# A two-layer encoder trunk: loading both embedding weights ahead of x, and taking rows 0-127 through the first projection first

## What is computed

```python
for i in range(DEPTH):                       # DEPTH = 2
    h = _rmsnorm(x, pre_norm_g[i])
    z = h @ w_in[i]                          # all groups' columns in one projection
    ...                                      # sparse and differential attention: oa, ob
    y = jnp.concatenate([oa * jax.nn.silu(ga), ob * jax.nn.silu(gb)], axis=-1) @ w_out[i]
    x = x + _rmsnorm(y, post_norm_g[i])
    gate = jax.nn.sigmoid(x @ w_ple_gate[i])
    e = (p[i] @ w_ple_proj[i]) * gate        # p: 256 rows by 256
    x = x + _rmsnorm(e, ple_norm_g[i])
```

## Time and profile before

| | |
|---|---|
| median of 3 runs | 394.84 us (394.23 to 395.21) |
| the profiled execution | 395.01 us |
| its span | 393.1 us |
| mean granted TensorE clock | 0.980 |
| PE busy | 367.1 us, 93% |
| DVE busy | 260.6 us, 66% |
| ACT busy | 222.3 us, 57% |
| POOL busy | 66.8 us, 17% |
| chain that ended last | PE 64%, DVE 11%, ACT 9%, DMA 5% |

### The profile page before, as it was taken

One profiled execution on the slowest core, in us unless ns is written; L12 is line 12 of the kernel. 1 busy time (PEld: TensorE's weight loads), 2 busy tenths in 40 slices (PEclk: granted clock), 3 DMA queues, 4 the chain that ended last, 5 costly groups with the idle time before them and its releaser, 6 DMA issues.

```text
span 393.1 us, 5602 instructions
## 1 busy us (share of the span) xinstructions
PE 367.1 (93%) x1932; PEld 301.6 (77%) x1932; DVE 260.6 (66%) x450; ACT 222.3 (57%) x451; POOL 66.8 (17%) x122
## 2 busy tenths in 40 slices
PE   6799999859999999999999999985999999999992
PEld 6597787748878788888888878774887878888882
DVE  2738697757766587588686579775666648757733
ACT  4838557662668645554674656766266855555321
POOL 1514331050400000003015513105041000000000
PEclk9999999997999999999999999999699999999998
DMA  7999735452455443667655753545235544352002
GB/s 267 303 234 334 251 96 174 136 159 81 111 155 166 158 162 111 182 214 138 204 171 173 252 160 91 178 131 161 84 99 170 160 162 154 113 179 90 0 23 85
DMA packets 32075, 61.64 MB, mean 157 GB/s; under 512 B 2384, under 2 KB 4688, under 8 KB 32048
## 3 DMA queue, kind: packets, MB, share of 16 engines
q1 hardware_dynamic: 30928, 58.01, 47.3%
q0 software_dynamic: 1120, 3.28, 4.1%
HBM read 60.23 MB, written 1.05 MB: 156 GB/s over the span
## 4 chain that ended last, share of the span: by engine, by line
PE 64%; DVE 11%; ACT 9%; DMA 5%; issue 5%; POOL 4%; SPq 1%; DVEq 0%; POOLq 0%; ACTq 0%
PE proj L932 17%; PE proj L933 17%; PE proj L934 17%; PE pv L1072 5%; DVE w_lo L689 4%; ACT w_hi L505 3%; DMA raw<-in_w_in_dram 3%; ACT probs L606 3%; DMA resid<-in_x_dram 2%; PE sc L974 2%; PE sc L1044 2%; PE tr L1057 2%; PE tr L990 1%; DVE score L767 1%; DVE neg_max L777 1%
## 5 line engine op out<-in xcount | busy, mean ns | idle before, releaser
L932 PE MATMUL proj<-w_hi,act_hi 128*128 128x512 f32 (+1 forms) x416 | 168.7, 406 | 0.9 <-DVE w_lo L689 0.8
L934 PE MATMUL proj<-w_hi,act_lo 128*128 128x512 f32 (+1 forms) x416 | 161.1, 387 | 0.0
L933 PE MATMUL proj<-w_lo,act_hi 128*128 128x512 f32 (+1 forms) x416 | 161.0, 387 | 0.0
L689 DVE TENSOR_TENSOR w_lo<-raw,w_hi 128x1024 fp32r<-128x1024 f32 (+1 forms) x108 | 129.2, 1212 | 38.8 <-ACT w_hi L505 38.2
L505 ACT ACTIVATE w_hi<-raw 128x1024 fp32r<-128x1024 f32 (+1 forms) x108 | 110.7, 1042 | 9.7 <-DMA raw<-in_w_in_dram 7.3
L932 PEld LDWEIGHTS proj<-w_hi,act_hi 128*128 128x128 f32 x416 | 79.0, 190 | 16.8 <-DVE w_lo L689 1.1
L934 PEld LDWEIGHTS proj<-w_hi,act_lo 128*128 128x128 f32 x416 | 78.8, 189 | 16.4
L933 PEld LDWEIGHTS proj<-w_lo,act_hi 128*128 128x128 f32 x416 | 79.1, 190 | 12.4
L606 ACT ACTIVATE probs<-sc,neg_max 128x128 f32<-128x128 f32 (+1 forms) x64 | 26.0, 426 | 31.1 <-DVE neg_max L777 31.1
L453 POOL TENSOR_TENSOR rstd<-var,minus_half 128x1 f32<-128x1 f32 x12 | 6.7, 556 | 192.1 <-DVE var L679 176.8
L1072 PE MATMUL pv<-v_all,pT 128*128 128x64 f32 (+1 forms) x144 | 20.5, 290 | 12.2 <-DVE qT_b L828 10.2
(11 more groups left out here) (124 smaller groups left out, 366.6 us busy)
## 6 DMA issues: line engine op xcount, KB each, us to landing
raw<-in_w_in_dram SPq DMA_DIRECT2D x64, 512.0 KB, 3.7
raw<-in_w_out_dram SPq DMA_DIRECT2D x16, 512.0 KB, 3.3
raw<-in_w_ple_gate_dram SPq DMA_DIRECT2D x16, 512.0 KB, 3.7
raw<-in_w_in_dram SPq DMA_DIRECT2D x8, 324.0 KB, 7.2
raw<-in_w_ple_proj_dram SPq DMA_DIRECT2D x4, 512.0 KB, 3.5
resid<-in_x_dram SPq DMA_DIRECT2D x2, 512.0 KB, 7.6
g_norm<-in_post_norm_g_dram POOLq DMA_DIRECT2D x2, 512.0 KB, 6.0
g_ple<-in_ple_norm_g_dram POOLq DMA_DIRECT2D x2, 512.0 KB, 7.5
```

The source lines that it names most:

```text
L689: nc.vector.tensor_tensor(w_lo[:, g % SLOTS, 0:nk * cols], raw[:, g % RAW_SLOTS, 0:nk * cols], w_hi[:, g % SLOTS, 0:nk * cols].bitcast(fp3 ...
L932: nc.tensor.matmul(ps, src_hi[:, b, k0 + k, :], hi, start=(first_u and k == 0), stop=False)
L933: nc.tensor.matmul(ps, src_hi[:, b, k0 + k, :], lo, start=False, stop=False)
L934: last = nc.tensor.matmul(ps, src_lo[:, b, k0 + k, :], hi, start=False, stop=last_k)
```

## The change

In SP's list of transfers the second embedding weight is put ahead of x's first block. The step "pre" is divided: "presq" holds ACT's part (the wait for x and the square), "pre" keeps the parts of DVE and POOL. In layer 0 all four embedding products come before the first transposes; block 0's square stands after mm(0,1), block 1's square after mm(1,1), and DVE's part of block 1's norm after the transposes of block 0. IDX then runs over units 2 to 5 for block 0, with block 1's transposes after unit 4, and then over units 2 to 5 for block 1. `START` is new for the first ten units. In layer 1 the two parts of "pre" stand next to each other, where "pre" stood.

```diff
-START = [1, 2, 5, 8, 11, 11, 16, 17, 18, 19]
+START = [1, 1, 7, 10, 11, 12, 15, 16, 18, 20]
...
     if L == 0:
-        out += [("pT", 0), ("pre", 0, 0)]
-        mms("PLE", ple, {0: [("pre", 1, 0)], 2: t8("h", 0), 3: t8("h", 1)})
-        mms("IDX", both, {})
+        out += [("pT", 0)]
+        mms("PLE", ple, {1: [("presq", 0, 0), ("pre", 0, 0)], 3: [("presq", 1, 0)] + t8("h", 0) + [("pre", 1, 0)]})
+        mms("IDX", one(0), {2: t8("h", 1)})
+        mms("IDX", one(1), {})
         mms("QB", both, {3: [("TI", 0)], 5: [("D", 0)]})
     else:
         out += [("ple0", 1, 1, L - 1)]
-        mms("PLE", ple, {0: t8("h", 0) + [("psq", 1, 1, L - 1), ("ple1", 1, L - 1)], 2: [("pre", 1, L)]})
+        mms("PLE", ple, {0: t8("h", 0) + [("psq", 1, 1, L - 1), ("ple1", 1, L - 1)], 2: [("presq", 1, L), ("pre", 1, L)]})
...
-                      12: ([("pre", 0, L + 1)] if L + 1 < DEPTH else []) + [("psq", 1, 0, L)]})
+                      12: ([("presq", 0, L + 1), ("pre", 0, L + 1)] if L + 1 < DEPTH else []) + [("psq", 1, 0, L)]})
...
-                if g == 0:
+                if g == 1:
                     load_x(0)
-                elif g == 1:
                     sp.dma_start(g_norm[:, :], pre_norm_g[0, :].partition_broadcast(P)).then_inc(gpre_in[0], 16)
                     load_x(1)
...
-                elif kind == "pre":
+                elif kind == "presq":
                     b, M = s[1:]
                     if M == 0:
                         act.wait_ge(x_in[b], 16)
```

## The result

| | before | after |
|---|---|---|
| median of 4 runs | 394.53 us (394.08 to 395.21) | 397.51 us (396.67 to 397.94) |
| profiled execution, its span | 395.01, 393.1 us | 396.67, 394.9 us |
| mean granted TensorE clock | 0.980 | 0.974 |

The ratio is 1.0072, with a 95% interval of 1.0056 to 1.0088: slower by 2.8 us by the ratio (3.0 between the two medians), where +1.7 was forecast.

The account below looks back on a forecast made before the run. TensorE, busy 93% of the span, was taken as the bound. Up to 1.0 us gained against 2.7 of new waits gave +1.73 us at the mark, carried to the end: 396.6 us, range 394.5 to 398.5.

Parts of the forecast that it names:

- The case that had half of the chances: The forecast itself: opening waits on PE move the end by +1.73 us to 396.6, own range 395.9 to 397.4; chance 0.50.
- Case C: Opening on PE: transposes and waits lower the clock, some 2 us on top of the waits, 398.7; chance 0.06.
- Case D: Unit 11's transfer lands late among POOL's loads, delaying TI's copy; D waits up to 2, likely 1: 397.7; chance 0.05.
- PE, embeddings; ACT, first rows: Opening: PE's 2.24 us gap goes, products end 13.6, not 17.0; square at 11.55; PE takes first norm at 14.87.
- ACT, second rows; DVE: Opening: square of rows 128-255 at 14.95; their norm at 19.5 to 20.8, delaying units 4 and 5's remainders behind it.
- the sum: Opening's total: up to 1.0 gained, 2.7 of new waits on PE; net +1.73 us.
- IDX and QB: PE after the embeddings: 0.9 us a half-unit, QB at 28.25 instead of 25.55, units 6 and 7 taking 5.47.
- The mark: Start on PE of QB's first product reading unit 8: 32.32 before, forecast 34.05; its shift moves the end equally.
- Case B: PE's two 5.12 us stalls: clock return gives 0.85 back twice, 395.0, chance 0.18; other way 398.3, 0.08.
- Case A: Opening: ACT and DVE less in the way, norm of rows 128-255 before 17.5, mark 31.35, 394.0; chance 0.10.
- Case E: SP's transfers: the swap does nothing, second weight lands at 9.3 as before, square 0.8 later: 397.4; chance 0.03.
- Layer 1: Second layer: both parts of "pre" adjacent, each engine's order the same, so no cost.

Follow-up runs that it names:

- experiment 2: after plus filler matmuls in PE's two opening gaps to keep the clock high; its 6-filler version, which gives QB at 28.46, measured 397.22 us, ratio 1.0058.
- swap_only: Kernel before with only the transfer swap, second embedding weight issued ahead of x's first block, step order as before; 395.34 us, ratio 1.0017.
- best version of experiment 7: early_sq_split plus filler matmuls ahead of PE's two long stalls; 387.49 us, ratio 0.9827 to before.
- after_fill20: after plus 20 filler matmuls on PE ahead of the 5.12 us wait in each layer; 392.85 us, ratio 0.9964 to before.
- sq_only: after with ACT's two squares alone moved ahead of the embedding copies that wait for PE, DVE's order kept; 397.53 us in one execution.
- early_sq_split: early_sq_hold, but the five small vectors issued after IDX's rotation of rows 128-255; 392.11 us, ratio 0.9931 to before.
- hold_loads: Kernel before with POOL's layer 0 loads issued only after QB's rotation of rows 128-255; 396.49 us, ratio 1.0052.
- early_sq_hold: after with squares early, norm of rows 128-255 ahead of unit 2's remainder, IDX alternating blocks, POOL's loads held; 394.18 us, ratio 0.9987.

## Why the prediction was right, and where it was off

The direction and the range held (397.51 in 394.5 to 398.5), and the forecast of +1.7 was too small by 1.1 us. The case that had half of the chances did not hold as it stood: 397.51 is above its own range (395.9 to 397.4), because two cases with 0.11 between them, C and D, came on top. Case C was priced at 398.7, outside of the stated range. That the time stayed inside is in part luck: C cost less than priced, and it and D overlap, as told below.

*PE, embeddings; ACT, first rows.* Right. Square at 11.57 (forecast 11.55), norm of rows 0-127 at 13.57 (13.55), transposes at 14.91 (14.87).

*ACT, second rows; DVE.* Right. Square 14.92 (14.95), norm of rows 128-255 19.34 to 20.62 (19.5 to 20.8), PE's wait for `act_lo` 1.41, then 1.03 for unit 4's remainder behind the norm (1.9 in the sum, less here because unit 3's products, at the low clock, took up a part of it).

*IDX and QB.* The term "0.9 us a half-unit" failed, because the rows it rests on were at the high clock. In after the matmuls of units 3 and 4 start 0.27 apart instead of 0.15. With the clock kept high, experiment 2 gives QB at 28.46, against 28.25 in the sum and 29.76 in after. The mark is then at 34.19, against 34.05 in the sum and 35.49 in after: 1.3 of the 1.4 us that the sum missed are the low clock's.

*Case C, the opening cools PE, 0.06.* It happened, at 1.3 us at TI instead of the 2 priced, and it deserved far more of the chance. I had written down 3.6 us of transposes and idleness, longer than the 2.24 us that left the clock alone, plus further waits, and yet called it unlikely. PE was idle for 1.15 and 1.41 us of it, with eight transposes in between, and the clock fell at about 19.0, after PE had resumed. The Trainium skill (TensorE: Matmul & The Clock Gate, Part 4) says that a transpose doesn't count as busy the way a matmul does. No run here settles that. In swap_only 2.65 us of idleness without a transpose lowered the clock too, so the idle time of after, 2.56 us in two parts, may be enough by itself. And in the best version of experiment 7, twelve transposes and an idle 1.45 us between the embedding products and unit 2 left the clock at 1.00:

```profile
13.64 1.03 PE L976 MATMUL sc<-ident,work 128*128 128x128 f32 x8
16.12 0.63 PE L976 MATMUL sc<-ident,work 128*128 128x128 f32 x4 [1.45 <-DVE act_lo L727]
16.82 0.39 PE L934 MATMUL proj<-w_hi,act_hi 128*128 128x324 f32 x1
```

*Case D, loads collide, 0.05.* It happened too. Unit 11's transfer took 10.1 us in after_fill20 and unit 11's copy started at 36.78 in after, with D at 38.43 just covered by PE; in sq_only D waited 1.63 us for it. The step that failed is "at the rate of before it lands at 33 to 34": while POOL's small vectors are in flight little is moved at a high share (80 GB/s at 0.87, as 38 at 0.78 in the earlier trace rows), so the bytes ahead are no measure of the time. That it is the small vectors and not POOL's large loads is seen in early_sq_split, where they were issued alone, from 31.15 to 34.1 us, the large loads from 40.91 on (columns as in rows 6):

```profile
36.00:38.00 2.00, 2.00 (x12) 1.60 (x11) 1.04 (x1) 1.28 (x2) 1.88 (x4) 1.00 0.97 28
```

The Trainium skill (Trainium Kernel Development and Optimization, Key Constraints) has all queues on the same 16 engines; hold_loads agrees, since unit 8 is no longer waited for once POOL's loads are out of its way.

C and D lie side by side, not in a row. In after TI's copy was ready for D at 38.22, held by unit 11, and PE's own work ended at about the same time, held back by the low clock. Where the low clock was absent or off PE's path, D was at 37.31, 37.48 and 38.13 in three executions, 0.3 to 1.1 us earlier and not 1.3, and the totals moved by 0.3 to 0.6. A version of after with both taken away and nothing else changed was not run.

*Case B, the clock gives it back.* It happened in the profiled execution. From the product behind the second layer's stall to the rotation's transposes it took 17.26 us in after (279.01 to 296.27) and 18.73 in before (275.83 to 294.56): 1.5 us less, hence the 1.7 of its total. Behind the first stall nothing was given back (18.47 in after, 18.30 in before). The medians don't show it (+3.0 with these stalls, +3.3 without their low clock), and behind the first stall the same stretch took 17.35 in early_sq_hold and 18.72 in early_sq_split, though each had one 5.12 us wait ahead of it. So it looks like a matter of the execution and not of the kernel; one profile of each kernel can't show it.

*Case A* did not occur: the norm ended at 20.62, not before 17.5. *Case E* did not either: the second weight's copy started at 8.07, in x's old place. *Layer 1*: the lag is 3.1 us at the first index product and 3.2 at the second layer's stall, so it cost nothing, as said.

## What to carry to other kernels

Before a step is put behind another on a busy engine, replay every engine's queue: here a copy that waits for PE came ahead of a square, and a norm with a round trip to POOL ahead of two weights, and the 2.24 us gap that went came back as waits of 1.15, 1.41 and 1.03. Durations from rows hold only at the clock of those rows: the clock stayed high behind an idle 2.24 us and fell behind 2.65, so a new gap of that length on PE must be priced with the matmuls behind it at half speed too, and filler matmuls that compute nothing are a cheap cover for a long stall (1.1% here, two lines). A load that is moved needs both questions asked: whom does it collide with, and who waits for it.

## What was not expected of the hardware

The two stalls of 5.1 us cost more by the clock behind them (4.4 us together) than the whole change did (2.8). In the opening the place at which the clock falls differs between executions of the same code: at about 17 us in one, 19 in another. Each filler, an f32 matmul of 128 by 128 by 128, ran as two records of about 0.12 us each. And the same 512 KB transfer took 3.7 us in the median but 10 to 12.7 us where the small broadcast vectors were in flight, with about 1 us of difference between executions.
